# Attention of each head group beside the next chunk's weights: one change to a decoder trunk kernel on one Trainium2 core

## What is computed

```python
q = rms_norm(proj[..., :N_HEADS * HEAD_DIM].reshape(B, T, N_KV, GROUP, HEAD_DIM), q_gain)
gates = sigmoid(proj[..., N_HEADS * HEAD_DIM:])            # three per head
s = einsum('bqgrd,bngd->bgrqn', qi, k_cmp) * scale - sl * d_cmp   # ALiBi: slope x distance
p_cmp = masked_softmax(s, d_cmp >= 0)
o_cmp = einsum('bgrqn,bngd->bqgrd', p_cmp, v_cmp)
...                                    # the same with k_slc, v_slc and with k_win, v_win
return g[:, :, 0] * o_cmp + g[:, :, 1] * o_slc + g[:, :, 2] * o_win     # then @ w_o
```

## Time and profile before

| | us |
|---|---|
| median of 3 runs | 2638.67 (2631.64 to 2641.95) |
| the profiled execution | 2634.83 |
| its span in the trace | 2633.1 |
| PE busy | 2538.1 (96%) |
| DVE busy | 2141.9 (81%) |
| ACT busy | 1246.5 (47%) |
| POOL busy | 379.2 (14%) |
| HBM traffic | 681.51 MB read, 260 GB/s over the span |
| mean granted clock of TensorE | 0.978 of full speed |

### The profile page before, as it was taken

How to read it: one execution, slowest core, us unless ns; L and a number is a source line. 1 busy time by engine, 2 the same in 40 slices (tenths; PEclk the granted TensorE clock), 3 DMA queues, 4 the chain that set the end, 5 groups by cost and what they waited for, 6 DMA issues and landing times.

```text
span 2633.1 us, 38477 instructions
## 1 busy us (share of the span) xinstructions
PE 2538.1 (96%) x14006; PEld 2179.7 (83%) x14006; DVE 2141.9 (81%) x2569; ACT 1246.5 (47%) x1638; POOL 379.2 (14%) x205
## 2 busy tenths in 40 slices
PE   5789999998999999999998999899899999999999
PEld 4678888887888888888887888688788888888887
DVE  7967998899999888988898987678989756665666
ACT  2254443544554355435544444573455435543553
POOL 0000110131120011101142300273112001100110
PEclk8899999999999999999999989899999999999999
DMA  9978688886778877787766877207677655555544
GB/s 379 380 289 337 261 330 333 330 325 243 297 276 306 323 264 287 294 336 272 284 254 244 313 286 291 113 1 288 248 286 267 237 192 182 185 192 180 188 175 144
DMA packets 94311, 685.49 MB, mean 260 GB/s; under 512 B 10465, under 2 KB 10465, under 8 KB 11233
## 3 DMA queue, kind: packets, MB, share of 16 engines
q1 hardware_dynamic: 93746, 681.27, 68.7%
q10 hardware_dynamic: 432, 2.38, 0.2%
HBM read 681.51 MB, written 2.10 MB: 260 GB/s over the span
## 4 chain that ended last, share of the span: by engine, by line
PE 86%; DVE 7%; DMA 4%; ACT 2%; issue 1%; POOL 0%; SPq 0%; DVEq 0%; ACTq 0%
PE banks L1422 51%; PE banks L1424 26%; DMA raw<-in_stream 4%; DVE raw L1064 3%; DVE w_lo L1048 2%; PE banks L1391 2%; PE banks L1393 2%; PE banks L1394 2%; PE banks L761 1%; ACT w_hi L901 1%; DVE temp L1117 1%; PE banks L725 1%; PE banks L747 1%; PE banks L1411 1%; DVE scratch L831 1%
## 5 line engine op out<-in xcount | busy, mean ns | idle before, releaser
L1422 PE MATMUL banks<-h_op,w_hi 128*128 128x512 f32 x3840 | 1359.7, 399 | 22.7 <-DVE h_op L1123 18.7
L1048 DVE TENSOR_TENSOR w_lo<-raw,w_hi 128x1024 fp32r<-128x1024 f32 x841 | 1092.4, 1322 | 354.1 <-ACT w_hi L901 350.2
L901 ACT ACTIVATE w_hi<-raw 128x1024 fp32r<-128x1024 f32 x841 | 876.8, 1056 | 1023.9 <-PE banks L1424 616.3
L1424 PE MATMUL banks<-h_op,w_lo 128*128 128x256 f32 x3840 | 1078.4, 281 | 0.0
L1422 PEld LDWEIGHTS banks<-h_op,w_hi 128*128 128x128 f32 x3840 | 725.0, 189 | 203.9 <-issue 23.6
L1422 PE MATMUL banks<-act_op,w_hi 128*128 128x512 f32 x2176 | 765.5, 397 | 0.1
L1424 PEld LDWEIGHTS banks<-h_op,w_lo 128*128 128x128 f32 x3840 | 728.2, 190 | 0.0
L1424 PE MATMUL banks<-act_op,w_lo 128*128 128x256 f32 x2176 | 608.9, 280 | 0.0
L1064 DVE CUSTOM_DVE_ANT_0 raw<-raw,c_all 128x2048 f32<-128x2048 f32 x224 | 552.1, 2484 | 15.0 <-ACT c_all L875 9.7
L1422 PEld LDWEIGHTS banks<-act_op,w_hi 128*128 128x128 f32 x2176 | 409.4, 188 | 99.9 <-DVE w_lo L1048 0.9
L1424 PEld LDWEIGHTS banks<-act_op,w_lo 128*128 128x128 f32 x2176 | 411.2, 189 | 0.0
(11 more groups left out here) (156 smaller groups left out, 1361.6 us busy)
## 6 DMA issues: line engine op xcount, KB each, us to landing
raw<-in_stream SPq DMA_DIRECT2D x645, 1024.0 KB, 5.4
x_res<-in_x SPq DMA_DIRECT2D x1, 2048.0 KB, 11.4
out_x<-x_res SPq DMA_DIRECT2D x4, 512.0 KB, 5.0
mix_area<-in_w_s ACTq DMA_DIRECT2D x1, 1024.0 KB, 4.9
mix_area<-in_b_s ACTq DMA_DIRECT2D x1, 1024.0 KB, 8.2
small<-in_small SPq DMA_DIRECT2D x1, 682.0 KB, 16.2
attn_area<-in_pos ACTq DMA_DIRECT2D x1, 273.0 KB, 5.4
c_all<-in_c SPq DMA_DIRECT2D x1, 8.0 KB
```

What stands on the lines that cost most here:

```text
L901: act.activation(w_hi[:, out, 0:n], raw[:, slot, half:half + n], ACT.Copy).then_inc(hi_ready, 1)
L1048: dve.tensor_tensor(w_lo[:, out, 0:n], raw[:, slot, half:half + n], w_hi[:, out, 0:n].bitcast(F32), ALU.subtract).then_inc(stream, 2 if ch ...
L1422: pe.matmul(banks[:, g + j, :], hi[:, k, P * j:P * (j + 1)], operand[:, kt, :], start=(kt == 0), stop=False, skip_group_check=True)
L1424: last = pe.matmul(banks[:, g + j, 0:T], lo[:, k, P * j:P * (j + 1)], operand[:, kt, 0:T], start=False, stop=(kt == last_kt), skip_group_c ...
```

## The change

- The phases become `kv`, `cmp`, `gate`, `q` (all four query chunks), `wo`. The input tiles `h_op` are now made during `cmp`. The modulation pieces stay 14 in number in this stretch (3 in `cmp`, 2 in `gate`, 3+2+2+2 in `q`), as do the weight pieces.
- The attention is cut into steps per head (both query halves together) and per group: sums (of squares of q), spread (the inverse root over 128 partitions), score, turn_cmp, turn (transpose), weigh (product with the values). Two tables, `PE_ATTENTION` and `SPLIT_ATTENTION`, put each step behind a sub: PE does it after the sub's matmuls, ACT and DVE after the sub's split. Group g runs in the chunk after its own query chunk and the beginning of the one after; group 3 runs in the first chunk of `wo`.
- The query is normalised once: PE spreads the inverse root with four 4-row matmuls of 256 columns, DVE multiplies the whole group (128 x 1024). ACT's scaling and DVE's separate maximum go: DVE reads the scores from PSUM in one `tensor_tensor_reduce` per branch and half, with a table of slope times distance that POOL builds per group. The compressed branch is handled once per group, with two transposes in place of eight, and its values stand four times in `vcmp`.
- The query chunks and `wo` chunk 0 write one sum into two banks in place of high and low sums in four (`one_sum`): three matmuls of 256 columns instead of one of 512 and one of 256. ACT copies the chunk and squares it at the first "E" of the next chunk; PE waits for that copy (`q_copied`) ahead of query chunks 2 and 3 and of `wo` chunk 0.

```diff
-            phases.append(("q", [Chunk("q", 0, "F3", ("q", 0))]))
-            phases.append(("cmp", [Chunk("cmp", 0, "P0", ("cmp", 0))]))
-            phases.append(("q1", [Chunk("q", 1 + i, "P3", ("q", 0)) for i in range(3)]))
+            phases.append(("cmp", [Chunk("cmp", 0, "F3", ("cmp", 0))]))
             phases.append(("gate", [Chunk("gate", 0, "G1", ("gate", 0))]))
+            phases.append(("q", [Chunk("q", i, "P2" if i else "P3", ("q", 0)) for i in range(4)]))
...
+PE_ATTENTION = {("q", 0, 0): ["keys"], ("q", 0, 2): ["cmp_keys"], ("q", 0, 4): ["spread_keys"],
+                ("q", 0, 6): ["gates"]}
+SPLIT_ATTENTION = {("q", 0, 3): ["keys"], ("q", 0, 5): ["cmp_keys"], ("q", 0, 7): ["spread_keys"],
+                   ("q", 1, 0): ["gates"]}
...
+    def pe(g, after, what, r=None):
+        c, u = divmod(after, 8)
+        key = ("q", g + 1 + c, u) if g + 1 + c < 4 else ("wo", g - 3 + c, u)
+        PE_ATTENTION.setdefault(key, []).append((what, g, r))
...
+    for g in range(3):
+        for after, what, r in ((0, "sums", None), (2, "spread", None), (3, "score", 0), (4, "score", 1),
+                               (5, "turn_cmp", None), (6, "turn", 0), (6, "score", 2), (7, "weigh", 0),
+                               (7, "turn", 1), (7, "score", 3), (8, "weigh", 1), (9, "turn", 2), (10, "weigh", 2),
+                               (10, "turn", 3), (11, "weigh", 3)):
+            pe(g, after, what, r)
+        for after, what, r in ((3, "sums", None), (5, "spread", None), (6, "score", 0), (7, "score", 1),
+                               (7, "scale", 0), (8, "turn_cmp", None), (8, "scale", 1), (9, "turn", 0),
+                               (9, "score", 2), (10, "turn", 1), (10, "weigh", 0), (10, "score", 3), (10, "scale", 2),
+                               (11, "weigh", 1), (11, "scale", 3), (12, "turn", 2), (13, "weigh", 2),
+                               (13, "turn", 3), (14, "weigh", 3)):
+            split(g, after, what, r)
+    for after, what, r in ((0, "sums", None), (1, "spread", None), (2, "score", 0), (3, "score", 1),
+                           (4, "score", 2), (4, "turn_cmp", None), (5, "score", 3), (5, "turn", 0),
+                           (5, "weigh", 0), (5, "turn", 1), (5, "weigh", 1), (6, "turn", 2), (6, "weigh", 2),
+                           (6, "turn", 3), (6, "weigh", 3)):
+        pe(3, after, what, r)
+    for after, what, r in ((3, "sums", None), (4, "spread", None), (5, "score", 0), (6, "score", 1),
+                           (6, "scale", 0), (7, "score", 2), (7, "turn_cmp", None), (7, "scale", 1),
+                           (8, "score", 3), (8, "scale", 2), (8, "turn", 0), (8, "weigh", 0), (8, "turn", 1),
+                           (8, "weigh", 1), (9, "scale", 3), (9, "turn", 2), (9, "weigh", 2), (10, "turn", 3),
+                           (10, "weigh", 3)):
+        split(3, after, what, r)
...
+            if cur.first.kind == "q" and cur.first.loc >= 2 or cur.first.source == ("wo", 0) and cur.first.loc == 0:
+                eng.wait_ge(q_copied, cur.first.loc if cur.first.kind == "q" else 4)
+                return
...
+            if what == "score":
+                dve.wait_ge(tables_built, g + 1)
+                dve.wait_ge(qk_done, n + 1)
...
+                    last = dve.tensor_tensor_reduce(
+                        part, banks[:, 4 + qb, keys * b:keys * (b + 1)], table(g, r)[:, T - keys:T], -1.0, 3e38,
+                        ALU.add, ALU.min, stat(n, NEG, k, 1))
...
+            if what == "turn_cmp":
+                pe.wait_ge(cmp_weights, g + 1)
...
+                if e == 0 and kind == "q":
+                    done_wait(act, prev)
...
+                    act.activation(q, banks[:, q_bank(prev.first):q_bank(prev.first) + 2, :].rearrange("p a t -> p (a t)"),
+                                   ACT.Copy).then_inc(q_copied, 1)
+                    act.wait_ge(q_copied, k + 1)
+                    act.activation(q_squares(k), q, ACT.Square).then_inc(queries_squared, 1)
...
                 if name == "wo":
-                    pe.wait_ge(out_lo, 4 * (u + 1))
+                    pe.wait_ge(out_lo, 2 * (u + 1))
...
+                                pe.matmul(out, hi[:, k, P * j:P * (j + 1)], operand[:, kt, 0:T],
+                                          start=(kt == 0 and j % 2 == 0), stop=False, skip_group_check=True)
+                                pe.matmul(out, hi[:, k, P * j:P * (j + 1)], operand[:, kt, T:HILO], start=False,
+                                          stop=False, skip_group_check=True)
+                                last = pe.matmul(out, lo[:, k, P * j:P * (j + 1)], operand[:, kt, 0:T], start=False,
+                                                 stop=(kt == KT - 1), skip_group_check=True)
```

More of the change, by code:

```diff
@@ L228 @@
+place_attention()
 class At:
@@ new lines, in prologue_act @@
+        def prologue_act(act, what):
+            if what == "keys":
+                act.wait_ge(cmp_done, 1)
+                for r in range(GRP):
+                    last = act.activation(vcmp[32 * r:32 * r + NCMP, :], banks[32 * r:32 * r + NCMP, 6, :], ACT.Copy)
+                act.activation(sq_c, banks[:, 5, 0:NB], ACT.Square).then_inc(cmp_keys_squared, 1)
+                act.wait_ge(square_sums, 1)
+                act.activation(r_k, banks[0:16, 7, 0:T], ACT.Sqrt, scale=1.0 / HD, bias=eps[0:16, :])                     .then_inc(rms_taken, 1)
+            if what == "cmp_keys":
+                act.wait_ge(square_sums, 2)
+                act.activation(r_c, banks[:, 5, 0:NB], ACT.Sqrt, scale=1.0 / HD, bias=eps[:, :]).then_inc(rms_taken, 1)
+            if what == "spread_keys":
+                act.wait_ge(zsum, BY_NAME["gate"][0].n["zsum"] + 1)
+                act.activation(gates_t, gates_t, ACT.Sigmoid).then_inc(gates_ready, 1)
@@ new lines, in attention_pool @@
+        def attention_pool(pool):
+            pool.wait_ge(h_ready, KT * (h_index("cmp") + 1))
+            pool.memset(spare[:, 1536:1792], 0.0).then_inc(cmp_zeroed, 1)
+            pool.wait_ge(pos_loaded, 32)
+            pool.wait_ge(cmp_done, 1)
+            build_table(pool, 0)
+            build_table(pool, 1)
+            for g in range(NKV):
+                for r in range(GRP):
+                    n = GRP * g + r
+                    pool.wait_ge(coef_ready, n + 1)
+                    for k, (qb, b, part) in enumerate(parts(n)):
+                        last = pool.tensor_scalar(part, part, stat(n, COF, k, 1), None, ALU.mult)
+                    last.then_inc(weights_scaled, 1)
+                if g < 2:
+                    build_table(pool, g + 2)
```

657 lines of the change are left out of this document (372 added, 285 removed).

## The result

The changed kernel takes 2689.14 us (median of 4 runs, 2685.63 to 2689.76) against 2635.52 (2631.64 to 2641.95) for the kernel before in the same comparison: the ratio is 1.0192, 95% interval 1.0177 to 1.0208. The forecast of 2657 had the sign and less than half of the size, and 2689 is outside its range of 2628 to 2682. The profiled execution took 2689.0 with a span of 2687.3, 54.2 more than the span before.

What follows compares the result with a forecast made beforehand. PE (TensorE) was taken to bound the kernel. Work of 322.5 us plus waits 30.9 and clock 6 gave 359.4 for the stretch, +22.2 against 337.2, so 2634.83 becomes 2657.0 us; range 2628 to 2682 (8 in 10).

Steps and rivals of the forecast that it cites:

- The sum without waits: PE's work from the end of `kv` to the end of `wo`: 322.5 us, 14.7 less than 337.2.
- Rival 1: All waits are covered by PE's weight products, together under 1.5 us: faster, 2620 us; chance 0.07.
- rival 4: Attention and weights don't overlap; excluded for the most part, the real part being group 3; no chance given.
- Rival 2: Half the waits: turn_cmp comes in time and the tail costs 7 us, giving 2641 us; chance 0.28.
- turn_cmp: PE reaches the transposes of the compressed weights before DVE has them: three waits of 2.0 us, 5.9 in all.
- to the first query product: `cmp` and `gate` after `kv`, `cmp` fitting beside the making of the input tiles: 36 us (32 to 41).
- chunk boundaries: PE waits for ACT's copy before query chunks 2 and 3 and `wo` 0: 3.9 us three times, 11.7.
- wait for POOL: No wait counted: POOL's four multiplications taken at 3.4 us, and POOL never named for long.
- group 3's waits: In the first `wo` chunk PE waits for scores, turns, copies of transposes and low parts: 13.3 us.
- lost at half clock: 6 us: 4 (0 to 12) for group 3 and the next weights, 2 for the start of the query weights.
- Rival 3: The clock falls at each of seven pauses, next 4 us of matmuls doing 2 of work: +14, 2671 us; chance 0.20.
- The signs named ahead: Trace signs: steady chunks about 46 + 6 us, POOL never named for long, clock 1.00 in query chunks 1 to 3.

Runs made afterwards that it cites:

- three_repairs: Changed kernel with ACT's boundary copy one sub earlier, a modulation piece moved earlier and 128-row spread matmuls: 2650.58 us, 1.0033 of the kernel before.
- copy_first: Changed kernel with ACT's copy of the previous chunk one sub earlier, in query chunks 1 to 3 and output chunk 0: 2671.46 us, 1.0127 of the kernel before.
- mods_early: Changed kernel with the last modulation piece of query chunks 1 to 3 moved behind the fourth sub: 2674.85 us, 1.0139 of the kernel before.
- act_scales: Changed kernel with ACT, not POOL, multiplying the weights of the first head of groups 0 to 2: 2670.64 us, 1.0096 of the kernel before.
- order_only: Kernel before with only the phases in the changed kernel's order, attention still one block ahead of `wo`: 2646.39 us, 1.0027 of the kernel before.
- after_again: The changed kernel, unaltered, measured once more: 2686.77 us, 1.0185 of the kernel before.
- wide_spread: Changed kernel with the spread of the inverse root contracting over 128 rows in place of 4: 2684.54 us, 1.0174 of the kernel before.
- repairs_tail: `three_repairs` with group 3's first copy ahead of a split and output chunk 0's last modulation piece moved earlier: 2646.09 us, 1.0035 of the kernel before.
- all_repairs: `repairs_tail` with the making of the input tiles spread over more splits of `cmp`: 2650.54 us, 1.0035 of the kernel before.

## Why the prediction fell short

**What bounds it, right.** PE is busy 0.96 of the span on either side, and its work didn't shrink. The sum without waits, 322.5, holds: `three_repairs` took 353.4; less 11.2 of idle time behind the first query product and less 15.4 lost at half clock there it is 326.8. The 4.3 above the sum are the terms that were off by work: in this trace 2.9 to the first query product, and as below +3.2, -2.3 and +0.6, together 4.4. Rival 1 (covered waits) and rival 4 (no overlap) are out. Rival 2 was right in one half: turn_cmp came in time.

Term by term, for the stretch of 384.5 against the forecast's 359.4:

| term | forecast | changed kernel | difference |
|---|---|---|---|
| to the first query product | 36 | 39.6 | +3.6 |
| 320 triples | 0.35 each | 0.36 | +3.2 |
| prologue | 12 | 9.7 | -2.3 |
| `wo` chunks 1 to 3 | 67.2 | 67.8 | +0.6 |
| chunk boundaries | 11.7 | 10.5 | -1.2 |
| turn_cmp | 5.9 | 0.9 | -5.0 |
| wait for POOL | 0 | 7.6 | +7.6 |
| group 3's waits | 13.3 | 10.2 | -3.1 |
| lost at half clock | 6 | 26.1 | +20.1 |
| not placed | | | +1.6 |

The 26.1 is half of PE's busy time at the lower level behind the first query product, 52.2 us, added up from the clock's records (the mean of 0.89 over the whole stretch, against 0.92 before, says the same more roughly).

**The step that failed most: the clock.** The sum had 2 for the start and 4 for group 3 (0 to 12), and nothing between. What the records show in the changed kernel, by what PE had done just before:

| clock at 0.50 behind | how often | us lost | forecast |
|---|---|---|---|
| the start of the query weights | 1 | 1.5 | 2 |
| the 4-row matmuls of a spread, PE busy | 4 of 4 | 6.9 | 0 |
| a wait for POOL, 2.5 us | 1 of 3 | 1.5 | 0 |
| a boundary's wait, 3.5 us | 3 of 3 | 8.6 | 0 |
| group 3's waits | 1 | 7.6 | 4 |

The first reason for the 0 was that a gap of 2.9 us had left the clock at 1.00. That row was one gap, and the clock fell only at 1564.1, 29 us behind it. In the changed kernel half clock followed one of the three waits for POOL, and every boundary, each of which stands 11 us behind a wait for POOL. The second reason was the reading of the prologue, whose 0.82 was put down to 7 us of idle time. The kernel before loses the clock there ahead of its pause, which begins at 1675.5, with PE busy in the 16-row spread of the keys (L700, from 1670.74):

```profile
1670.70:1673.30 2.60, 2.60 (x13) 2.22 (x13) 1.92 (x2) 2.16 (x3) 0.00 (x0) 1.00 0.00 0
1673.30:1675.50 2.20, 2.20 (x8) 1.63 (x6) 0.10 (x1) 0.00 (x0) 0.00 (x0) 0.50 0.00 0
```

The prediction had seen that this spread "ran as the clock fell", and took from it a price for the new spreads themselves, and none for the products behind them.

Rival 3 (0.20) had the mechanism for the pauses, with 2 us for each of seven, 14, and its 2671 was the nearest of the four. The pauses' part was 13.7 above the forecast (8.6, 1.5 and 3.6), but the nearness is in part luck: three of its seven pauses, those for the compressed weights, were 0.3 us or less, the boundaries cost 2.9 each, and the 6.9 behind the spreads stood in no rival. The Trainium skill's rule (TensorE: Matmul & The Clock Gate, "HAM oscillation") tells of bursts between waits that each start at the slow clock. The traces agree for the three boundaries, and `copy_first` shows it there by removal. They don't agree for two of the three waits for POOL, behind which the clock stayed at 1.00, and the falls behind the spreads have no wait ahead of them. What the traces add is that the same pause of 3.5 us can cost 2.3 or 1.4 us behind it.

**The step that failed next: POOL.** "3.4 of 4.27" was the price of four multiplications beside a DVE that worked on scores. The change puts them beside weight splits and a modulation reduction. I had costed what POOL does and not who reads SBUF beside it, and wrote that POOL would never be named for long; it was waited for 2.5 us three times, 7.6. `mods_early` and `act_scales` show it.

**turn_cmp** came in time. DVE's new reduce of a head is four instructions; in order of time, the first, the last and what follows:

```profile
1637.72 0.28 DVE L686 CUSTOM_DVE_ANT_0 temp<-banks,mix_area 128x128 f32<-128x128 f32 x1
...
1638.48 0.42 DVE L686 CUSTOM_DVE_ANT_0 temp<-banks,mix_area 128x256 f32<-128x256 f32 x1
1638.83 0.08 DVE L686 DVE_READ_ACCUMULATOR2_ANT temp<- 128x1 f32 x1
1638.83 0.17 DVE L709 TENSOR_SCALAR temp<-temp 128x4 f32<-128x4 f32 x1
...
1639.97 0.28 DVE L729 TENSOR_TENSOR temp<-temp 128x120 f32<-128x120 f32 x1
```

1.1 us (forecast 1.65, bounds 0.9 to 2.2), twice in the chain, and 1.4 for the eight small steps (1.6): 1.3 of the 1.7 by which each wait was shorter. The rest I didn't take apart.

**Boundary and group 3** were right as mechanisms: three waits of 3.5 us for the forecast's 3.9, and 10.2 us of waits in group 3 for 13.3. **The table switches of ACT**, which the sum put at nothing, cost nothing that shows: there are 11 loads of 1.28 us in the stretch (4 before), and none in the chain of the first boundary (1657.2 to 1660.7).

**To the first query product** the order costs more than I took it for. `order_only` shows 38.1 for it where the sum has 36; 2.5 more of its 5.9 are the wait ahead of the attention, which the changed kernel doesn't have, and 1.3 I can't place. I had placed `cmp` "beside the making of the input tiles" and let it fit; its products wait for splits between the tiles.

**The 256-column products**: 0.360, against my 0.35, which is 3 us of the 5 kept for the range.

**The signs named ahead.** Four came out against the forecast: chunks of 58 and not 52, POOL waited for, the clock at 0.91 in query chunks 2 and 3 and not at 1.00, and the first query product at 1577.9, later than 1573 (6.1 us of it lie ahead of the stretch).

## What to carry to other kernels

Where the bounding engine is TensorE and it is already busy, as here, laying small dependent steps between its products buys pauses. Each is to be costed with what the clock does behind it; here a pause with another one 11 us ahead of it cost more than the same pause alone. And small matmuls of few rows are to be costed with the clock behind them too. When a step moves, ask not only how long its engine takes for it but what the neighbour that shares its path to SBUF will be doing at that time. The wait at the boundary was a matter of one place in an order: two strings changed by one sub gave back 15 of some 50 us, and three small edits 36.

## What the runs showed that I had not expected

**Two paces of the same products at full clock.** Groups of like instructions on PE between 300 and 400, where the code is the same; first the kernel before, then the changed kernel:

```profile
L1422 PE MATMUL banks<-h_op,w_hi 128*128 128x512 f32 x166 | 57.6, 394 | 0.0
L1424 PE MATMUL banks<-h_op,w_lo 128*128 128x256 f32 x166 | 46.0, 277 | 0.0
```

```profile
L1605 PE MATMUL banks<-h_op,w_hi 128*128 128x512 f32 x166 | 58.7, 399 | 0.0
L1607 PE MATMUL banks<-h_op,w_lo 128*128 128x256 f32 x166 | 46.6, 281 | 0.0
```

The same 166 products take 57.6 or 58.7 us (0.347 or 0.353 us each from start to start), at a granted clock of 1.00. The pace holds for hundreds of us and changes within a run: between 800 and 900 the kernel before has 399 ns as well. It goes with the execution and not with the kernel: in the other traces the slower pace prevails, and the profiled execution of the kernel before is one of its quick ones (2634.8, with medians of 2636 to 2641 in the later comparisons). That fits the 6 us ahead of the touched stretch, and part of the difference between the 54 us in the profiles and the 49 in `after_again`'s comparison. What sets the pace stays open.

**Narrow matmuls and the clock.** Over the five traces in which the spreads have 4 rows and the rest varies (the two of the changed kernel, `copy_first`, `mods_early` and `act_scales`), the granted clock was at 0.50 for 3.4 us behind 15 of 20 spreads, with PE busy throughout. Over the four in which they have 128 rows (`wide_spread`, `three_repairs`, `repairs_tail`, `all_repairs`) it stayed at 1.00 behind all sixteen. `wide_spread` differs from the changed kernel in nothing else and has the same pauses, so that the number of rows matters here. It isn't all that matters, since five of the 20 had no fall behind them, and what made the difference for these stays open.
